# Experts' loop of a decoder layer: written out, gathering by eight experts into windows of slots, gates turned with the one-hots

## The reference, cut to what matters

```python
def layer_norm(x, g, b):
    xf = x.astype(jnp.float32)
    mu = jnp.mean(xf, axis=-1, keepdims=True)
    var = jnp.mean(jnp.square(xf - mu), axis=-1, keepdims=True)
    return ((xf - mu) * lax.rsqrt(var + NORM_EPS) * g.astype(jnp.float32) + b.astype(jnp.float32)).astype(x.dtype)

def moe_ffn(x, w_router, router_bias, w_exp_gu, w_exp_down, w_sh_gu, w_sh_down):
    t = x.reshape(-1, d)
    scores = jax.nn.sigmoid(jnp.dot(t, w_router).astype(jnp.float32))
    choice = scores + router_bias.astype(jnp.float32)
    grp = choice.reshape(n_tok, N_EXPERT_GROUPS, N_EXPERTS // N_EXPERT_GROUPS)
    grp_score = jnp.sum(lax.top_k(grp, 2)[0], axis=-1)
    _, top_g = lax.top_k(grp_score, TOP_GROUPS)
    ...
    _, idx = lax.top_k(jnp.where(emask, choice, -jnp.inf), TOP_K)
    w = jnp.take_along_axis(scores, idx, axis=-1)
    w = w / jnp.sum(w, axis=-1, keepdims=True) * ROUTED_SCALE
    gates = jnp.zeros((n_tok, N_EXPERTS), jnp.float32).at[jnp.arange(n_tok)[:, None], idx].set(w).astype(t.dtype)
    gu = t @ w_sh_gu
    y = (jax.nn.silu(gu[:, :SHARED_FF]) * gu[:, SHARED_FF:]) @ w_sh_down
    for e in range(N_EXPERTS):
        gu = t @ w_exp_gu[e]
        h = jax.nn.silu(gu[:, :EXPERT_FF]) * gu[:, EXPERT_FF:]
        y = y + gates[:, e:e + 1] * (h @ w_exp_down[e])
    return y.reshape(b, s, d)

def reference(...):
    ...
        x = layer_norm(DN_ALPHA * x + moe_ffn(x, ...), ln3_g[l], ln3_b[l])
```

## Time and profile before

| what | us |
|---|---|
| median of three runs | 1071.47 (1071.45 to 1071.48) |
| the profiled execution's own time | 1072.56 |
| its span in the trace | 1070.4 |
| TensorE busy | 1040.8 |
| VectorE busy | 524.6 |
| ScalarE busy | 376.0 |

### The profile page before, as it was taken

One profiled execution on the slowest core, in us unless ns is written; L12 is line 12 of the kernel. 1 busy time (PEld: TensorE's weight loads), 2 busy tenths in 40 slices (PEclk: granted clock), 3 DMA queues, 4 the chain that ended last, 5 costly groups with the idle time before them and its releaser, 6 DMA issues.

```text
span 1070.4 us, 16979 instructions
## 1 busy us (share of the span) xinstructions
PE 1040.8 (97%) x6816; PEld 762.5 (71%) x6817; DVE 524.6 (49%) x983; ACT 376.0 (35%) x662; POOL 57.3 (5%) x53
## 2 busy tenths in 40 slices
PE   8999999999999999999999999999999999999995
PEld 7999999999999999999865445545544555445452
DVE  6998456676789966755852222122211222222223
ACT  5655535555675643454311111111111111111112
POOL 0002003243000000000200000000000000000000
PEclk9999999999999999999999999999999999999998
DMA  7664443343443456469589999999985999999912
GB/s 291 210 224 158 158 150 126 126 145 126 148 167 123 154 184 216 157 254 414 195 307 406 417 402 420 382 409 406 415 359 229 398 417 419 414 386 397 415 62 79
DMA packets 41644, 290.72 MB, mean 272 GB/s; under 512 B 4712, under 2 KB 5872, under 8 KB 6896
## 3 DMA queue, kind: packets, MB, share of 16 engines
q1 hardware_dynamic: 40800, 284.62, 68.2%
q0 software_dynamic: 784, 5.24, 1.3%
HBM read 288.78 MB, written 1.06 MB: 271 GB/s over the span
## 4 chain that ended last, share of the span: by engine, by line
PE 85%; DVE 10%; ACT 2%; issue 2%; DMA 1%; SPq 0%; ACTq 0%; DVEq 0%
PE stream L1466 22%; PE stream L1796 21%; PE stream L1822 11%; PE stream L1491 8%; PE stream L1737 6%; PE work L1785 6%; DVE w_lo L949 3%; DVE acc L986 2%; DVE rms L1112 2%; DMA raw<-in_wdense 1%; PE stream L1808 1%; PE work L1592 1%; PE work L1568 1%; PE stream L1815 1%; PE work L1674 1%
## 5 line engine op out<-in xcount | busy, mean ns | idle before, releaser
L949 DVE TENSOR_TENSOR w_lo<-raw,w_hi 128x1024 fp32r<-128x1024 f32 x142 | 171.1, 1224 | 54.0 <-ACT w_hi L657 53.9
L1796 PE MATMUL stream<-ring,xg 128*64 128x512 f32 x640 | 197.2, 593 | 0.2 <-issue 0.2
L657 ACT ACTIVATE w_hi<-raw 128x1024 fp32r<-128x1024 f32 x142 | 147.0, 1051 | 55.0 <-DMA raw<-in_wdense 40.1
L1466 PE MATMUL stream<-xT_hi,w_hi 128*128 128x256 f32 x560 | 160.4, 286 | 1.3 <-DVE w_lo L949 1.3
L1466 PE MATMUL stream<-xT_lo,w_hi 128*128 128x256 f32 x560 | 157.9, 282 | 0.0
L1466 PE MATMUL stream<-xT_hi,w_lo 128*128 128x256 f32 x560 | 157.8, 282 | 0.0
L1796 PEld LDWEIGHTS stream<-ring,xg 128*64 128x64 f32 x640 | 64.7, 137 | 88.8 <-issue 88.8
L1466 PEld LDWEIGHTS stream<-xT_hi,w_hi 128*128 128x128 f32 x560 | 106.1, 189 | 6.1 <-issue 3.5
L1357 DVE TENSOR_TENSOR hh<-h,stream 128x256 f32<-128x256 f32 x32 | 13.5, 422 | 196.9 <-ACT h L878 196.9
L1466 PEld LDWEIGHTS stream<-xT_hi,w_lo 128*128 128x128 f32 x560 | 105.9, 189 | 0.0
L1466 PEld LDWEIGHTS stream<-xT_lo,w_hi 128*128 128x128 f32 x560 | 105.6, 189 | 0.2 <-issue 0.2
(11 more groups left out here) (364 smaller groups left out, 2092.0 us busy)
## 6 DMA issues: line engine op xcount, KB each, us to landing
ring<-in_wstream SPq DMA_DIRECT2D x120, 1024.0 KB, 9.3
raw<-in_wdense SPq DMA_DIRECT2D x73, 1024.0 KB, 4.8
place_e<-in_wstream SPq DMA_DIRECT2D x24, 1024.0 KB, 9.4
place_m<-in_wstream SPq DMA_DIRECT2D x12, 1024.0 KB, 9.0
place_c<-in_wstream SPq DMA_DIRECT2D x12, 1024.0 KB, 10.6
place_w<-in_wstream SPq DMA_DIRECT2D x12, 1024.0 KB, 8.5
place_x<-in_wstream SPq DMA_DIRECT2D x12, 1024.0 KB, 10.1
ln<-in_lnp POOLq DMA_DIRECT2D x3, 1024.0 KB, 7.0
```

Source lines behind the costliest of these rows:

```text
L657: nc.scalar.activation(w_hi[:, q % ROUNDED, :], raw[:, q % 6, :], ACT.Copy).then_inc(w_rounded, 1)
L949: tt(w_lo[:, q % 6, :], raw[:, q % 6, :], w_hi[:, q % ROUNDED, :].bitcast(F32), ALU.subtract).then_inc(w_rest, 1)
L1466: last = mm(S[n % 4][:, 0:SEQ], w[:, b, :], a[:, kb, :], start=(kb + j == 0), stop=(kb == chunks * KB - 1 and j == len(parts) - 1))
L1796: last = mm(S[2][e * SLOTS:(e + 1) * SLOTS, :], x[:, kb, col + e * SLOTS:col + (e + 1) * SLOTS], tiles[e][kb // 4][:, kb % 4 * 512:(kb % 4 ...
```

## The change

1. **The loop is written out.** `Fori` goes on all engines: 32 pairs stand one behind the other, and each pair's scatter but the last one's comes behind the next pair's gate-up.
2. **Groups of eight.** `PER_GROUP` is 8: a gather fills one bank with one feature block of eight experts, 512 columns. A group's one-hots now serve four pairs, two feature blocks being gathered in each. The last four pairs gather nothing.
3. **Windows of slots.** Tokens of the first block fill an expert's slots from 1 upwards, those of the second from 64 downwards, and each block may reach 48 of them. Of a gather's four matmuls the first runs over all 512 columns and the other three over 8 x 48 = 384. What doesn't fit goes to the overflow path by a new table (`slot_over`, `ranks`), made while the loop begins.
4. **Gates ride with the identity.** `turner` holds the identity and behind it the pair's two gates as high and low part; one matmul of 132 columns for each token block takes the place of one with the identity and one f32 matmul with the gates. VectorE adds the pieces of a slot's gate up (`tensor_reduce`) and fills in the next pair's gates (`make_gates`).
5. **Sums.** `shared_down` moves behind the first gate-up and opens the sums itself; the residual is added by VectorE into the banks in pair 0; `bound_sums` ahead of the loop goes, and the one behind it becomes `end_sums`, two matmuls of two columns.

```diff
-PER_GROUP = 4
-ROUND = 8
+PER_GROUP = 8
+WINDOW = 48
+LAST_GROUP = PAIRS - PER_GROUP // 2
...
+        window = (slice(0, WINDOW), slice(SLOTS - WINDOW, SLOTS))
+        unused = (slice(WINDOW, SLOTS), slice(0, SLOTS - WINDOW))
...
-        zero_r = sb("zero_r", [P, P], A + 4 * KIB, F32R)
-        ident_r = sb("ident_r", [P, P], A + 5 * KIB + 512, F32R)
-        xg = [sb(f"xg{b}", [P, KB, PER_GROUP * SLOTS], H + 8 * KIB * b) for b in range(2)]
+        TURN = P + 4
+        turner = sb("turner", [P, TB, TURN], BESIDE + 2 * KIB, F32R)
+        xg = [[sb(f"xg{b}_{half}", [P, KB // 2, PER_GROUP * SLOTS], o) for half, o in enumerate(place)]
+              for b, place in enumerate(((H, DEAD), (H + 8 * KIB, G)))]
...
             refilled = PAIRS - 1 - RING // 3
-            with sp.Fori(0, refilled // ROUND) as k:
-                for j in range(ROUND):
-                    refill(k * ROUND + j, 3 * j % RING, k * (3 * ROUND) + (RING + 3 * j))
-            for pair in range(refilled // ROUND * ROUND, refilled):
+            for pair in range(refilled):
                 refill(pair, 3 * pair % RING, RING + 3 * pair)
...
+            for t in range(TB):
+                zeros = ones[:, 0:SLOTS - WINDOW].unsqueeze(1).to_broadcast([P, 2 * PER_GROUP, SLOTS - WINDOW])
+                tt(onehot[:, :, t, :, unused[t]], zeros, zeros, ALU.subtract)
+
+            ve.wait_ge(router_mm, 3)
+            in_block = [W[2][:, t * EXPERTS:(t + 1) * EXPERTS] for t in range(TB)]
+            n_first = W[2][:, 2 * EXPERTS:3 * EXPERTS]
+            from_top, free = over[0][:], over[1][:]
+            link(ts(from_top, in_block[1], -1.0, SLOTS + 1.0, ALU.mult, ALU.add))
+            link(stt(free, n_first, float(WINDOW), from_top, ALU.min, ALU.is_lt))
+            link(tt(free, free, sel[:, 1, :], ALU.mult))
+            tt(slot_of[:, 0, :], in_block[0], sel[:, 0, :], ALU.mult)
+            tt(slot_of[:, 1, :], from_top, free, ALU.mult).then_inc(place_done, 1)
...
-                    tt(onehot[:, buf, t], slot_no.unsqueeze(1).to_broadcast([P, PER_GROUP, SLOTS]),
-                       slot_of[:, t, first].unsqueeze(2).to_broadcast([P, PER_GROUP, SLOTS]), ALU.is_equal
+                    tt(onehot[:, buf, t, :, window[t]],
+                       slot_no[:, window[t]].unsqueeze(1).to_broadcast([P, PER_GROUP, WINDOW]),
+                       slot_of[:, t, first].unsqueeze(2).to_broadcast([P, PER_GROUP, WINDOW]), ALU.is_equal
                        ).then_inc(onehot_done, 1)
...
+            def make_gates(pair):
+
+                gates = gates_e[:, :, 2 * pair:2 * pair + 2]
+                link(nc.vector.tensor_copy(turner[:, :, P:P + 2], gates))
+                tt(turner[:, :, P + 2:P + 4], gates, turner[:, :, P:P + 2].bitcast(F32), ALU.subtract
+                   ).then_inc(gates_done, 1)
...
+                for c in range(2):
+                    r = slice(c * SLOTS, (c + 1) * SLOTS)
+                    nc.vector.tensor_reduce(slot_gate[r, :], by_block[r, :, P + c:TURN:2], AX.XY, ALU.add
+                                            ).then_inc(gate_cp, 1)
+                nc.vector.tensor_copy(scatT[:].rearrange("p (t c) -> p t c", t=TB), by_block[:, :, 0:P]
+                                      ).then_inc(scatT_cp, 1)
+                if pair + 1 < PAIRS:
+                    make_gates(pair + 1)
...
+                if pair == 0:
+                    ve.wait_ge(shared_mm, 1)
+                    for t in range(TB):
+                        for c in range(2):
+                            cols = slice(c * 512, (c + 1) * 512)
+                            bank = W[2 * t + c][:]
+                            link(stt(bank, x2h[:, t, cols].bitcast(F32), ALPHA, bank, ALU.mult, ALU.add))
+                            stt(bank, x2l[:, t, cols].bitcast(F32), ALPHA, bank, ALU.mult, ALU.add
+                                ).then_inc(residual_done, 1)
...
+            def gather(kb, bank, buf):
+
+                by_expert = bank[:].rearrange("p (e s) -> p e s", e=PER_GROUP)
+                w = slice(kb * P, (kb + 1) * P)
+                mm(by_expert, x2h[:, 0, w], onehot[:, buf, 0], start=True, stop=False, skip_group_check=True)
+                mm(by_expert[:, :, window[0]], x2l[:, 0, w], onehot[:, buf, 0, :, window[0]], start=False, stop=False,
+                   skip_group_check=True)
+                mm(by_expert[:, :, window[1]], x2h[:, 1, w], onehot[:, buf, 1, :, window[1]], start=False, stop=False,
+                   skip_group_check=True)
+                mm(by_expert[:, :, window[1]], x2l[:, 1, w], onehot[:, buf, 1, :, window[1]], start=False, stop=True,
+                   skip_group_check=True).then_inc(gath_mm, 1)
...
-            bound_sums(True)
...
+            def end_sums():
 
                 for t in range(TB):
-                    for c in range(2):
-                        for x in (x2h, x2l):
-                            mm(W[2 * t + c][:], alpha_ident, x[:, t, c * 512:(c + 1) * 512].bitcast(F32),
-                               start=False, stop=False, skip_group_check=True)
+                    mm(W[2 * t + 1][:, 0:2], turner[:, 0, 0:P], onehot[:, 0, 0, PER_GROUP - 1, WINDOW:WINDOW + 2],
+                       start=False, stop=True, skip_group_check=True).then_inc(moe_mm, 1)
...
+            def turn_onehot(buf, col):
 
                 for t in range(TB):
-                    mm(S[0][:, t * P:(t + 1) * P], onehot[:, buf, t].rearrange("p e s -> p (e s)")[:, col:col + P],
-                       ident_r[:], start=True, stop=True)
-                for t in range(TB):
-                    last = mm(S[0][:, SEQ:SEQ + 2],
-                              onehot[:, buf, t].rearrange("p e s -> p (e s)")[:, col:col + P].bitcast(F32),
-                              gates(t), start=(t == 0), stop=(t == TB - 1))
-                last.then_inc(done, 1)
+                    last = mm(S[0][:, t * TURN:(t + 1) * TURN],
+                              onehot[:, buf, t].rearrange("p e s -> p (e s)")[:, col:col + P], turner[:, t, :],
+                              start=True, stop=True)
+                last.then_inc(scatT_mm, 1)
...
+            for pair in range(PAIRS):
+                buf, col = pair // 4 % 2, (pair % 4) * P
+                if pair % 4 == 0:
+                    pe.wait_ge(gath_act, 4 + pair)
+                    pe.wait_ge(gath_dve, 4 + pair)
...
+                gate_up(buf, col, [places[expert_tile(pair, e)] for e in range(2)], gu_mm, landed)
+                if pair == 0:
+                    shared_down()
+                else:
+                    if pair == 1:
+                        pe.wait_ge(residual_done, 4)
+                    pe.wait_ge(yl_done, 2 * pair)
+                    scatter()
...
+                turn_onehot(buf, col)
+                if pair < LAST_GROUP:
+                    pe.wait_ge(onehot_done, 2 * (pair // 4) + 4)
+                    gather(2 * (pair % 4), S[1], (buf + 1) % 2)
...
+                if pair < LAST_GROUP:
+                    gather(2 * (pair % 4) + 1, S[0], (buf + 1) % 2)
...
-            bound_sums(False, moe_mm)
+            end_sums()
```

More of the change, by code:

```diff
@@ L1730, in turn_shared @@
                 last.then_inc(hsT_mm, 1)
-            def gather(block, bank, buf, done):
-                parts = [(x, t) for t in range(TB) for x in (x2h, x2l)]
-                for b in range(2):
-                    for k, (x, t) in enumerate(parts):
-                        last = mm(bank[:, b * SEQ:(b + 1) * SEQ], x[:, t, (block + b) * P:(block + b + 1) * P],
-                                  onehot[:, buf, t].rearrange("p e s -> p (e s)"),
-                                  start=(k == 0), stop=(k == len(parts) - 1))
-                last.then_inc(done, 1)
@@ L1742, in _ @@
-            pe.wait_ge(onehot_done, 3)
-            pe.wait_ge(split_l, 2)
-            for k in range(4):
-                if k < 2:
-                    turn_shared(k)
-                    pe.wait_ge(sh_silu, k + 1)
-                gather(2 * k, S[k], 0, gath_mm)
-            pe.wait_ge(hsT_cp, TB + 1)
-            pe.wait_ge(wsd_ld, 16)
-            pe.wait_ge(place_done, 2)
-            def bound_sums(first, done=None):
-                for t in range(TB):
-                    for c in range(2):
-                        last = mm(W[2 * t + c][:], zero_r[:],
-                                  onehot[:, 0].rearrange("p t e s -> p (t e s)"),
-                                  start=first, stop=not first, skip_group_check=True)
-                    if done is not None:
-                        last.then_inc(done, 1)
@@ L1765, in shared_down @@
+            pe.wait_ge(onehot_done, 2)
+            pe.wait_ge(split_l, 2)
+            for kb in range(KB):
+                if kb < 2:
+                    turn_shared(kb)
+                    pe.wait_ge(sh_silu, kb + 1)
+                elif kb >= 4:
+                    pe.wait_ge((gath_act, gath_dve)[kb % 2], (kb - 4) // 2 + 1)
+                gather(kb, S[kb % 4], 0)
```

(43 more changed lines are left out.)

217 lines of the change are left out of this document (99 added, 118 removed).

## The result

The changed kernel takes **1034.18 us** (median of four runs, 1033.51 to 1034.81) where the one before takes 1071.47: a ratio of 0.9656 [0.9644, 0.9668], 37.3 us faster. The profiled execution ran 1034.76 us with a span of 1032.5.

What follows compares the result with a forecast made beforehand. TensorE, busy 97% of the span, was taken to bound the kernel. Savings of 16.2 + 6.2 + 6.1 + 6.9 - 3.0 + 0.4 = 32.8 us gave 1039.8 from the profiled 1072.56, by the median 1038.7 us, range 1031 to 1048.

Steps and rivals of the forecast that it cites:

- A, pairs with gathering: In 28 of 32 pairs, shorter turning and gathers take 0.58 us off each, 16.2 us together.
- The path that sets the second gather's end: Down waits for ScalarE's hT, 1.29 to 1.44 us from the first gather's last matmul; the second gather just not held up.
- B, the last four pairs: These pairs gather nothing, and down waits for scatT: 1.54 us saved in each, 6.2 us together.
- C, round ends: With the loop written out, three of four round ends go, at 2.03 us each: 6.1 us.
- D, the residual: In pair 0 the residual leaves TensorE and hides on VectorE with 1.9 us to spare: 6.9 us saved.
- E, ahead of the loop: Before the first gate-up, longer VectorE work and the gathers of eight blocks cost 3.0 us.
- The stream: Weight transfers at 406 GB/s fall behind the 427 wanted, but the last half lands eight us before the last down.
- (1): Weight stream binds in the loop: at 3% under 406 GB/s the last half lands late, 1045 us; chance 0.10.
- (2): In gathering pairs, strided 384-column matmuls cost what 512 do, or scatT comes late: 1044 to 1047 us; chance 0.11.
- (3): More gain in pairs, by a short hT signal and no register instructions: a pair 14.5, total 1032 us; chance 0.13.
- (4): Loop code fetched in a line beside the full stream makes it slower: 52 us if exposed, 1091 us; chance 0.02.
- (5): Windows of 48 slots send some pair to the overflow path, 30 us each, 1069 with one; chance 0.02.

Runs made afterwards that it cites:

- gates_apart: Changed kernel with the gates' part undone: gates by their own f32 matmuls again, slot gates copied, no splitting on VectorE; 1045.43 us.
- h_first: Changed kernel with ScalarE copying hT before the first gathered bank instead of after it; 1034.58 us.
- swap: Changed kernel with two banks exchanged: second gather fills S[3], down's first half S[0], the wait for scatT standing behind the gather; 1032.93 us.
- swap_h: Changed kernel with the second gather's and down's banks exchanged and hT copied ahead of the gathered bank; 1029.27 us.
- best3: swap_h with windows of 40 slots instead of 48; 1025.75 us.
- thin3: swap_h with gathers of two matmuls instead of four, leaving out the tokens' low parts; 1022.50 us.
- wide: Changed kernel with all four matmuls of a gather over 512 columns instead of one of 512 and three of 384; 1041.62 us.
- round_ends: Changed kernel, straight code, with the scatter of pairs 7, 15 and 23 ahead of the next gate-up again; 1041.90 us.
- best: h_first with windows of 40 slots, and the wait for scatT only where a gather follows it; 1030.51 us.
- thin_h: h_first with gathers of two matmuls instead of four, leaving out the tokens' low parts; 1024.10 us.

## Why the prediction was right

It said 1038.7 (1031 to 1048); 1034.18 was measured, 4.5 us less. The mechanism held: TensorE's pieces add up, and what left TensorE left the time. The saving was sized 12% too small (32.8 of 37.3), and two of its numbers came out right by luck, as said at each. Of the profiled executions' difference of 37.8 us, the loop and what follows give 39.6 (524.1 to 484.5), and the stage ahead takes 1.8 back.

- **A, pairs with gathering.** Right in kind, undersized: 0.71 a pair for 0.58, 19.9 us for 16.2. This is the step with most of the error. Of the 0.13, 0.06 is in the first gather. I had kept "the 0.1 by which the first gather is longer than the second". But 0.06 of it belonged to the f32 matmuls of the gates in front of it: its first matmul has 0.28, and 0.34 in gates_apart, where they stand again. Turning was 0.02 less than taken, scatter 0.02 less, and the second gather fell by 0.05 for 0.03.
- **The path that sets the second gather's end.** The step said that down would wait for hT, 1.29 to 1.44 behind the first gather's last matmul. It was 1.38 (752.66 to 754.04), so the number held; but the reason was half of it, and that is luck. By the step the second gather was "just not held up" at the copies' price. It was held by 0.14 at this very price (two reductions 0.35, the two copies 0.34 in the earlier trace rows): VectorE starts when the turning ends, and the first gather and the turning of h, which cover it, take 1.03 where they took 1.28. h_first, swap and swap_h show both waits ending together.
- **B, the last four pairs.** 13.65 for 13.77: 6.6 us for 6.2. That down waits for scatT there is shown by its four waits. The gathers of experts that don't exist were not put back, so B isn't tested alone.
- **C, round ends.** 6.1 forecast. Between the traces three round ends gave 5.8, at 1.94 each; putting only the scatters back cost 7.3. The size held to 0.3; of the 2.03 that it took for each, 0.09 lie outside the first round's end. The cause is the scatter's order alone.
- **D, the residual.** 6.9 forecast, 6.87 in pair 0, in the open on TensorE and hidden on VectorE, with 3.1 us to spare (yl done 571.66, scatter at 574.75) for the 1.9 I gave it: the eight operations on PSUM took 0.69 and 0.70 each and 5.3 together, not 0.75 and 6.2.
- **E, ahead of the loop.** -3.0 forecast and measured. The common start is the product that forms the gates, at 533.76 in the kernel before and 532.57 after:

```profile
532.57 0.29 DVE L1304 TENSOR_TENSOR gates_e<-scores,sel 128x128 f32<-128x128 f32 x1
```

  From there the first gate-up came 12.51 us later before, 15.48 now, 2.97 more. That the sum is exact is luck: up to the first turning on TensorE 0.63 was added for the 0.9 forecast, and from there to gate-up 2.34 for 2.1. No run tries these terms apart. That the product itself came 1.2 earlier is part of the surplus. In the changed kernel and all its variants it comes between 531.2 and 532.9, and the one trace of the kernel before is of an execution 1.1 over that kernel's median, so I count it as variation; this isn't shown.
- **The stream.** It was said to fall behind and to end with 8 us in hand, for the last half and the last down. There it had 9.8: the last half landed at 1003.3 for 1010, and the last down began at 1013.1 for 1018. The tightest half was another, of the last gate-up, with 7.1, and the step didn't look at it. Over all 176 halves the stream made 411 GB/s for the 406 taken; its full pace is 420, and what it moved more slowly up to 620 us takes the rest. The 406 of the earlier trace rows held such slow stretches as well: where that window is cut in 40 slices, they read 210 to 431 GB/s. I weighed it against 358 GB/s from the Trainium skill (DMA: Bandwidth & Descriptors, Where 436 GB/s comes from) and read that as a bound for this core. The same page of the Trainium skill, under Measured (HBM→SBUF, 128 partitions, SWDGE, issued from GpSimd), keeps 358 for two cores that stream at once and has 425 GB/s for a core alone with 16 MB. This kernel runs on one core, and its 420 GB/s over 240 us lie 1% under that figure. Even so that figure would not have given the last landing: an estimate with it, 552.8 + 3 + 176 x 2.47, is 990, further off than 1010, since it has no pause in it.

**The rivals.** (1), the stream binds: no wait for a landing in the loop, but the reserve was down to 7.1 us, and best3 and thin3 use it up. (2), dear columns: out by wide; late scatT is real, but small, 0.14 a pair. (3), more gain, is nearest in time, 1032, but not in its reason. The first pieces did shrink, the gather's by 0.06 and scatter by 0.02, but gates_apart, straight code too, has the gather's 0.06 back, so it belongs to the gates' matmuls and not to register instructions; and the pair stopped at 14.60, not 14.5. (4), code: seven packets more, no 'issue' piece inside a pair, and round_ends in straight code loses more, not less, than the old loop. Its 52 us didn't come. (5), overflow: 32 silus ran, as before, so no pair took that path.

Of the marks set beforehand the pieces 6.87, 2.07, 0.20, 0.87, 0.22, 0.8 to 0.9 and 3.58 read 6.87, 2.05, 0.18, 0.81, 0.22, 0.90, 3.58; gate-up 0 stands at 548.05 for 549.3 (1.2 of it upstream); the last pairs take 13.65 for 13.8.

## What to carry to other kernels

Where one engine is busy all the time, a sum of its pieces forecast a pair to 0.01 us in gates_apart and to 0.13 for the whole change, and missed by 0.18 (best) and 0.43 (thin_h) where another engine's result came too late. And two waits that end at the same moment must be taken away together: each experiment that moves only one of them reads as "it isn't this one". Ask of every shortened stretch which other engine's result is due right behind it, since a saving in front of a fixed path turns into a wait. And before more is taken off the engine, work out the pace of the stream and the depth it lives on; the depth hides a shortfall for hundreds of microseconds and then gives all of it back.

## What the runs showed of the hardware

- The weights' stream went at 420 GB/s with 1 MB halves in every long window without a pause, in the changed kernel and in thin3, whether TensorE waited or not. The 423 of the earlier trace rows is from 10 us, where slices scatter around that pace.
- A matmul whose moving operand leaves out slots (8 x 48 or 8 x 40 of 8 x 64) costs by the columns that it moves: 0.175 us for 384, in best3 0.14 to 0.15 for 320, where 512 in a row cost 0.235.
- The first matmul behind plain f32 ones took 0.34, behind the 132-column one 0.28, with the same 512 columns (gates_apart against the changed kernel; what makes it so wasn't tried).
